# Seven block products in place of eight for one 512x1024x1024 projection, with the weight sums made on GpSimd

## What is computed

```python
a = nsa_attention(...) @ w_branch_attn               # 512 -> 1024
b = pool_mixer(u_pool, ...) @ w_branch_pool          # 512 -> 1024
ga, gb = jnp.split(jax.nn.sigmoid(g_merge), 2, axis=-1)
x = x + (ga * a + gb * b) @ w_out                    # the second output projection, 1024 -> 1024
h = rms_norm_2(x, norm_mlp)
return x + jnp.square(jax.nn.relu(h @ w_ff1)) @ w_ff2
```

## Time and profile before

| | |
|---|---|
| three runs | 1021.49, 1021.76, 1024.25 us |
| profiled execution: its own time | 1022.31 us |
| its span in the trace | 1020.3 us |
| PE busy | 1006.6 us of the span |
| second output projection, first matmul to the first one of the MLP | 637.40 to 683.63 us |
| split tiles of the MLP, to the first whole one | 683.63 to 698.17 us |

### The profile page before, as it was taken

How to read it: one execution, slowest core, us unless ns; L and a number is a source line. 1 busy time by engine, 2 the same in 40 slices (tenths; PEclk the granted TensorE clock), 3 DMA queues, 4 the chain that set the end, 5 groups by cost and what they waited for, 6 DMA issues and landing times.

```text
span 1020.3 us, 14242 instructions
## 1 busy us (share of the span) xinstructions
PE 1006.6 (99%) x5158; PEld 827.6 (81%) x5158; DVE 681.2 (67%) x1201; ACT 555.2 (54%) x1013; POOL 419.1 (41%) x403
## 2 busy tenths in 40 slices
PE   9999999999999999999999999999999999999997
PEld 7788877778778898878887788888888888888886
DVE  5678898888984256733577889344323325999997
ACT  7455444777862456544667874224433446554555
POOL 0023012666720003900354520008779865875563
PEclk9999999999999999999999999999999999999999
DMA  9533321337140384132200443249999941443552
GB/s 338 105 98 93 104 62 42 84 84 197 53 175 1 123 282 131 47 98 63 63 2 1 155 164 96 83 134 311 355 356 340 356 168 62 154 136 143 207 186 83
DMA packets 100165, 146.24 MB, mean 143 GB/s; under 512 B 6480, under 2 KB 60496, under 8 KB 100096
## 3 DMA queue, kind: packets, MB, share of 16 engines
q1 hardware_dynamic: 86800, 130.75, 39.6%
q10 hardware_dynamic: 12768, 12.88, 3.9%
q0 software_dynamic: 528, 1.70, 1.0%
HBM read 123.69 MB, written 21.63 MB: 142 GB/s over the span
## 4 chain that ended last, share of the span: by engine, by line
PE 88%; DVE 6%; ACT 2%; issue 1%; DMA 1%; SPq 1%; POOL 0%; ACTq 0%; DVEq 0%
PE bank L968 59%; PE bank L1483 5%; PE bank L1485 5%; PE bank L1484 5%; PE bank L1363 2%; PE bank L1150 2%; PE bank L1372 2%; PE bank L1121 2%; DVE x L2249 1%; PE bank L1386 1%; PE bank L1134 1%; DMA arena<-in_x 1%; DVE stats L2248 1%; DVE u_lo L2151 1%; PE bank L1273 1%
## 5 line engine op out<-in xcount | busy, mean ns | idle before, releaser
L2666 DVE TENSOR_TENSOR w_lo<-wring,w_hi 128x1024 fp32r<-128x1024 f32 x32 | 51.4, 1607 | 107.5 <-ACT w_hi L2004 107.5
L2151 DVE TENSOR_TENSOR u_lo<-wring,u_hi 128x1024 fp32r<-128x1024 f32 (+2 forms) x69 | 83.3, 1215 | 52.8 <-ACT u_hi L1657 52.3
L968 PE MATMUL bank<-u_hi,h_hi 128*128 128x512 f32 (+1 forms) x288 | 110.9, 385 | 0.0
L968 PE MATMUL bank<-u_hi,h_lo 128*128 128x512 f32 (+1 forms) x288 | 109.2, 379 | 0.0
L968 PE MATMUL bank<-u_lo,h_hi 128*128 128x512 f32 (+1 forms) x288 | 109.0, 378 | 0.0
L1657 ACT ACTIVATE u_hi<-wring 128x1024 fp32r<-128x1024 f32 (+1 forms) x64 | 66.0, 1033 | 70.4 <-PE bank L968 54.5
L968 PE MATMUL bank<-h_hi,w_hi 128*128 128x512 f32 (+2 forms) x272 | 103.2, 379 | 0.0
L968 PE MATMUL bank<-h_hi,w_lo 128*128 128x512 f32 (+2 forms) x272 | 103.1, 379 | 0.0
L968 PE MATMUL bank<-h_lo,w_hi 128*128 128x512 f32 (+2 forms) x272 | 103.1, 379 | 0.0
L968 PE MATMUL bank<-h_hi,u_hi 128*128 128x512 f32 x224 | 93.4, 417 | 0.4 <-ACT arena L1599 0.2
L968 PE MATMUL bank<-h_hi,u_lo 128*128 128x512 f32 x224 | 88.2, 394 | 0.0
(11 more groups left out here) (401 smaller groups left out, 2596.6 us busy)
## 6 DMA issues: line engine op xcount, KB each, us to landing
wring<-in_w_in SPq DMA_DIRECT2D x60, 512.0 KB, 3.9
wring<-in_w_ff ACTq DMA_DIRECT2D x12, 1024.0 KB, 8.5
wring<-sums_kept SPq DMA_DIRECT2D x16, 768.0 KB, 4.2
wring<-in_w_ff SPq DMA_DIRECT2D x22, 512.0 KB, 6.3
wring<-in_w_ff SPq DMA_DIRECT2D x32, 256.0 KB, 3.3
sums_kept<-wring SPq DMA_DIRECT2D x22, 256.0 KB, 5.2
wring<-in_w_out SPq DMA_DIRECT2D x2, 2048.0 KB, 13.0
wring<-in_w_ff SPq DMA_DIRECT2D x4, 1024.0 KB, 6.9
```

Of the source, the lines that this page charges most:

```text
L968: last = mm(b, lhs, rhs, start=(start and n == 0), stop=(stop and n == 2))
L2151: done = v.tensor_tensor(u_lo[raw_place(u)][:, cols], raw_unit(u)[:, cols], u_hi[hi_place(u)][:, cols].bitcast(F32), ALU.subtract)
L2666: v.tensor_tensor(cut(w_lo[ring3(m)]), src, cut(w_hi[ring3(m)]).bitcast(F32), ALU.subtract).then_inc(w_lo_done, 1)
```

## The change

The projection C = A W, with A the mixed activations (two halves of 256 tokens, two halves of 512 inner rows) and W cut into four quarters B11, B12, B21, B22 of 512x512, is made with seven products instead of eight (Winograd's form of Strassen's scheme). With A11, A12 the two inner halves of the first 256 tokens and A21, A22 those of the last: S1 = A21+A22, S2 = S1-A11, S3 = A11-A21, S4 = A12-S2; T1 = B12-B11, T3 = B22-B12, T2 = B22-T1, T4 = B21-T2. The products, in the order in which PE makes them, are B11 with A11, T2 with S2, T1 with S1, B22 with S4, B21 with A12, T3 with S3, T4 with A22. Each has two tiles of tokens (t = 0, 1), four chunks and three matmuls: 24 matmuls of 512 columns, 168 in all.

*Weight sums.* POOL makes T1, T2, T3 and T4 under the first output projection, in eight sets of 512 KB. SP loads a set into one of three places, POOL makes four sums of 128x256, SP stores the set in DRAM (`sets_kept`), waits for the store, and loads the next set into that place. All of this stands in SP's list ahead of the loads of the second layer, and in POOL's list ahead of three memsets for the second layer. The quarters are read back during the branch products.

*Sides.* S1 to S4 are made by DVE (`side_work`, in 256 columns) in the last four rounds of the branch loop, and split by ACT and DVE like the other operands.

*Adds.* A product adds into up to three of the four blocks of x. DVE adds the banks, ACT copies the first product to a running sum, and POOL adds the running sum to x (`add_running`, six adds of 128x512).

*MLP.* The first two tiles are split in 256 and 256 columns, and the transposes of tokens 256 to 511 come inside them.

```diff
@@ SP @@
+            def load_set(s):
+                by_half = lambda a: a.rearrange("p (n c) -> p n c", n=2)[:, :, s % 2 * 2 * P:(s % 2 + 1) * 2 * P]
+                for h in range(2):
+                    row = (4 * h + s // 2) * P
+                    sp.dma_start(set_place[s % SET_PLACES][:, 2 * h:2 * h + 2, :], by_half(w["w_out_2"][row:row + P, :])).then_inc(set_in[s % SET_PLACES], 16)
+            def keep_set(s):
+                sp.wait_ge(set_summed, SET_SUMMED + 4 * (s + 1))
+                sp.dma_start(sets_kept[s].rearrange("p (q c) -> p q c", q=4), set_place[s % SET_PLACES]).then_inc(set_kept[s % SET_PLACES], 16)
...
+                    for s in range(SETS):
+                        keep_set(s)
+                        if s + SET_PLACES < SETS:
+                            sp.wait_ge(set_kept[s % SET_PLACES], SET_KEPT + 16 * (s // SET_PLACES + 1))
+                            load_set(s + SET_PLACES)
...
+                        if e == 3:
+                            sp.wait_ge(last_lo_done, 2)
+                            load_quarter("T1")
+                        elif e == 5:
+                            load_quarter("B21")
+                        elif e == 6:
+                            sp.wait_ge(mix_done, 4)
+                            load_quarter("T2")
+                        elif e == 7:
+                            load_quarter("T3")
+                            load_quarter("T4")
@@ PE @@
+            def out2(name, t):
+                if name in out2_behind:
+                    pe.wait_ge(r_free, out2_behind[name] + t)
+                q = seven.index(name)
+                for j in range(4):
+                    if t == 0 and j % 2 == 0:
+                        pe.wait_ge(w2o_lo_done, low_count(name, j // 2))
+                    if isinstance(out2_sides[name], str):
+                        if t == 0 and j == 0:
+                            pe.wait_ge(side_lows, SIDE_LOWS + ("S2", "S1", "S4").index(out2_sides[name]) + 1)
...
+                        if t == 0 and name in ("B11", "B21"):
+                            pe.wait_ge(m_lo_done, (0 if name == "B11" else 4) + j + 1)
...
+            for name in seven:
+                for t in range(2):
+                    out2(name, t)
+                if name == "T3":
+                    for i in range(2):
+                        h3(i)
...
+            ff_tile(0, 0, 2 * P, range(3))
+            h3(2)
+            ff_tile(0, 0, 2 * P, range(3, KC))
+            h3(3)
...
+            ff_tile(1, 0, 2 * P)
             pe.wait_ge(h_lo_done, halves("h3", NT - 1, 1) + 1)
             for c in range(2):
-                ff_tile(c, 3 * P, S).then_inc(a_full, 1)
+                ff_tile(c, 2 * P, S).then_inc(a_full, 1)
@@ ACT @@
+                quarter_high(*EARLY_HIGHS[e])
+                if e >= 4:
+                    act.wait_ge(mix_done, e + 1)
+                    run(m_hi[e][:, :], gaT[:, e, :], ACT.Copy).then_inc(m_hi_done, 1)
+                    act.wait_ge(side_sums, SIDE_SUMS + 3 * (e - 4) + 2)
+                    run(m_hi[e - 4][:, :], gaT[:, e - 4, :], ACT.Copy).then_inc(m_hi_done, 1)
@@ DVE @@
+            def side_work(j):
+                upper, lower, other = gaT[:, j, 0:2 * P], gaT[:, j, 2 * P:S], gaT[:, j + 4, 2 * P:S]
+                s1, s2 = side_part(side_raw["S1"], j), side_part(side_raw["S2"], j)
+                dve.wait_ge(mix_done, j + 5)
+                v.tensor_tensor(s1, lower, other, ALU.add).then_inc(side_sums, 1)
+                v.tensor_tensor(lower, upper, lower, ALU.subtract).then_inc(side_sums, 1)
+                dve.wait_ge(side_sums, SIDE_SUMS + 3 * j + 1)
+                v.tensor_tensor(s2, s1, upper, ALU.subtract).then_inc(side_sums, 1)
+                mixed2_low(j)
...
+            LOW_AT = {1: (("B11", 0),), 2: (("B11", 1),), 3: (("B22", 0),), 6: (("T2", 0),), 7: (("T2", 1), ("T1", 0))}
...
+                if e >= 4:
+                    side_work(e - 4)
+                for name, h in LOW_AT.get(e, ()):
+                    quarter_low(name, h)
@@ POOL @@
+            for s in range(SETS):
+                pool.wait_ge(set_in[s % SET_PLACES], 32 * (s // SET_PLACES + 1))
...
+                g.tensor_tensor(b11, b12, b11, ALU.subtract).then_inc(set_summed, 1)
...
+            all_kept(pool)
             pool.wait_ge(xn_done, NT)
...
+            def add_running(i, n, t):
+                xs = x[:, i, n * 512:(n + 1) * 512]
+                g.tensor_tensor(xs, xs, running[t], ALU.add).then_inc(running_added, 1)
```

More of the change, by code:

```diff
@@ L134, in weight_groups @@
     groups += [("block2", [])]
-    groups += [(f"w2o{n}", [cols(w["w_out_2"], 512 * n, 512)]) for n in range(2)]
+    groups += [(f"w2o{n}", []) for n in range(2)]
     return groups
@@ new lines, in build @@
+        side_hi = {name: half(f"side_hi{n}", SIDE, ("hT", n * SIDE)) for n, name in enumerate(("S1", "S2", "S4"))}
+        running = [wring[:, 3 * SLOT + S * t:3 * SLOT + S * (t + 1)] for t in range(2)]
+        side_part = lambda a, j: a[:, 2 * P * j:2 * P * (j + 1)]
+        HIGHS = ("B11", "B22", "T1", "T2", "B21", "T3", "T4")
+        high_count = lambda name, h: 2 * HIGHS.index(name) + h + 1
+        LOWS = [("B11", 0), ("B11", 1), ("B22", 0), ("T2", 0), ("T2", 1), ("T1", 0), ("T1", 1), ("B22", 1)]
@@ L506, in build @@
+        LOWS += [(name, h) for name in ("B21", "T3", "T4") for h in range(2)]
+        low_count = lambda name, h: LOWS.index((name, h)) + 1
+        SETS, SET_PLACES = 8, 3
+        set_place = [region(4 * 2 * P, at).rearrange("p (q c) -> p q c", q=4) for at in (strips_at, strips_at + 8 * P, zT_at + 2 * S)]
+        set_slot = {"T1": 0, "T3": 1, "T4": 2, "T2": 3}
         unit_at = [16384, 18560, 18560 + 2 * D]
@@ L957, in t_bank, with three @@
                 return bank[4 + n % 2]
-            def three(b, weights, cols, act, rows, weights_first, start, stop, terms=range(3)):
+            def three(b, weights, cols, act, rows, weights_first, start, stop, terms=range(3), low_at=None):
                 (w_high, w_low), (a_high, a_low) = weights, act
+                low_cols = cols if low_at is None else slice(low_at, low_at + cols.stop - cols.start)
                 for n, (wt, a) in enumerate(((w_high, a_high), (w_high, a_low), (w_low, a_high))):
@@ L964, in three @@
                         continue
[L965 removed]
+                    lhs, rhs = wt[:, low_cols if n == 2 else cols], a[:, rows]
                     if not weights_first:
@@ new lines, in _ @@
+            out2_behind = {"B11": R_OUT2 - 1, "B21": out2_used("T2") - 1, "T3": out2_used("T2") - 1, "T4": out2_used("T3") - 1}
+            def out2(name, t):
[8 more added lines that the diff above has]
+                            pe.wait_ge(side_lows, SIDE_LOWS + ("S2", "S1", "S4").index(out2_sides[name]) + 1)
+                        side = side_hi[out2_sides[name]], side_lo[out2_sides[name]]
+                        rows = slice((2 * j + t) * P, (2 * j + t + 1) * P)
+                    else:
+                        highs, lows, at = out2_sides[name]
+                        if t == 0 and name in ("B11", "B21"):
+                            pe.wait_ge(m_lo_done, (0 if name == "B11" else 4) + j + 1)
+                        side = highs[j], lows[j]
+                        rows = slice(at + t * P, at + (t + 1) * P)
+                    last = three(bank[out2_bank[name] + t][:, :], (w2o_hi[q % 4], w2o_lo[name, j // 2]), slice(512 * j, 512 * (j + 1)), side, rows,
+                                 False, j == 0, j == 3, low_at=j % 2 * 512)
+                last.then_inc(r_full, 1)
@@ L1449, in _, with ff_tile @@
             h3 = lambda i: h_transposes("h3", xn3, 2 * NT, [i])
-            residual(R, ready2, product2, h3)
-            R += 2 * NT
-            def ff_tile(c, first, end):
-                for k in range(KC):
+            def ff_tile(c, first, end, chunks=range(KC)):
+                for k in chunks:
                     last = three(bank[AT[("ff", c)] % 2][:, first:end], (w_hi[ring3(c)], w_lo[ring3(c)]), slice(k * P, (k + 1) * P),
@@ new lines, in out2_add @@
+            def out2_add(name, t):
+                part = bank[out2_bank[name] + t][:, :]
+                dve.wait_ge(r_full, R_OUT2 + 2 * seven.index(name) + t + 1)
+                xs = lambda i, n: x[:, i, n * 512:(n + 1) * 512]
+                if name == "T2":
+                    dve.wait_ge(first_copied, FIRST_COPIED + t + 1)
+                elif name == "T3":
+                    dve.wait_ge(running_added, RUNNING_ADDED + t + 1)
+                elif name == "T1":
+                    v.tensor_tensor(xs(2 + t, 1), xs(2 + t, 1), part, ALU.add)
+                    dve.wait_ge(running_added, RUNNING_ADDED + t + 1)
+                elif name == "B22":
+                    dve.wait_ge(r_free, out2_used("T1") - 1 + t)
+                elif name == "B21":
+                    dve.wait_ge(r_free, out2_used("B11") - 1 + t)
+                elif name == "T4":
```

(3 more changed lines are left out.)

279 lines of the change are left out of this document (211 added, 68 removed).

## The result

Eight runs of the changed kernel have a median of 1023.92 us (1023.12 to 1025.81), eight of the kernel before 1021.62. The ratio is 1.0021, with an interval of 1.0012 to 1.0030. The forecast was 1020.8, that is 1.0 us faster. The time lies in the range, and within 0.3% of before, but on the other side, and the interval leaves out no change.

A forecast was written before the change was run, and what follows sets the result against it. It took PE's own list as the bound. Gross gain 7.7 less entry 2.9, transfers 1.3, T2 1.2 and tail 1.3 left 1.0 us less, forecast as 1020.8 us; range 1017.0 to 1024.4.

The forecast's parts named there:

- The gross gain of 7.7 us: PE's list: 24 fewer matmuls in the second output projection, 5.45 us, and the MLP tiles cut at 256 columns, 2.25.
- the entry wait: Before B11's fourth chunk: PE waits 2.9 us for DVE's low part, behind the last gate, S1 and S3; 1.8 to 3.3.
- the wait at T2: Before product T2: PE waits 1.2 us for S2's low part on DVE, 0.6 to 1.3; sign: ended by L2850.
- the sets and the third `kwvg` unit: Eight weight-sum sets ahead of the second layer's loads: cost nothing, at most 0.6 us; no PE wait for that unit.
- a wait at (4, 1) behind T1's load: Sign in the timeline: a PE wait of 1 to 2 us at branch product (4, 1), ended by its weights' low part.
- The late set loop: Rival: stores landing in 7.5 us, not 4.7, make the third `kwvg` unit 7 us late; 6 slower, 1026.8; chance 0.07.
- the tail, term (4): From T4's end into the MLP: waits before transposes and last low part, 1.3 us; floor 0.5, ceiling 2.5 with GpSimd contention.
- term (2): Transfers: T1's 1 MB ahead of branch piece 4 delays product (4, 1); rows give 1.5 us, 1.3 taken, 0 to 2.6.
- The clock was a rival: Rival: behind the entry wait the clock drops to 1.2 of 2.4 GHz for 24 matmuls; 4.4 slower, 1026.2; chance 0.05.
- a slice below full: Sign that the prediction was wrong: a granted clock below full in any slice of the profile.

The follow-up runs named there:

- experiment 2: Changed kernel with GpSimd's four last adds (running sums into x, tokens 256 to 511) cut from 512 to 8 columns: 1022.48 us, ratio 1.0010.
- experiment 1: Changed kernel with T1's 1 MB load issued behind branch piece 4, not ahead of it: 1022.33 us, ratio 1.0007.
- experiment 7: Changed kernel with the edits of experiment 6 together with T1's load behind branch piece 4: 1022.53 us, ratio 1.0006.
- experiment 5: Changed kernel with 26 more useless 512-column matmuls on PE, set in front of four of its waits: 1023.29 us, ratio 1.0014.
- Experiment 3: Changed kernel with A11's fourth chunk split into high and low parts two rounds earlier, so B11 no longer waits for S3: 1024.18 us, ratio 1.0023.
- experiment 6: Changed kernel with A11's fourth chunk split early and DVE's list behind the last gate set by need, S2 first: 1023.42 us, ratio 1.0019.
- version 12: Experiment 9's kernel with T4's first add before the second h_lo pair, the second MLP tile's weight low part later, two early running adds on DVE: 1018.16 us.
- experiment 10: Experiment 9's kernel with all six running adds on DVE and none on GpSimd: 1020.62 us, ratio 0.9985.
- experiment 9: Experiment 7's kernel with norms and T3's first add ahead of the MLP's weight differences, and one of B22's earlier: 1019.63 us, ratio 0.9977.

## Why the prediction was wrong

*What held.* The gross gain of 7.7 us; the entry wait, 2.73 for 2.9; the wait at T2, 1.13 for 1.2, ended by the low part of S2 (L2856; the L2850 that the prediction names, and that ends DVE's list in the section on the change, is S4 ahead of it); the sets and the third `kwvg` unit, hidden; a wait at (4, 1) behind T1's load. The late set loop did not happen; 6 slower would have been 1027.8 and not 1026.8.

*The step that failed is the tail, term (4).* It was put at 1.3 with a ceiling of 2.5, and it was 3.74. The sum took the add, the norm and the transposes as the tail's chain and found short waits there. The runs show another: DVE's first two differences of h_lo, which the first MLP tile needs, at 1.61 us each beside GpSimd's adds (0.64 alone, experiment 2), a wait of 1.66, and 1.7 us at the lower clock behind it. The row for the contention was at hand, 2.19 for 1.22 in the earlier trace rows, but the 1.3 holds nothing for it: it was given to "two or three DVE steps of the tail" in the ceiling alone, and to none that PE waits for ahead of the first tile.

The Trainium skill, "GPSIMD Engine Reference", section "1. Specifications", names VectorE instructions with two SBUF inputs among those that contend with GpSimd, and experiment 2 agrees on both sides: the differences slow down by 2.5 times, the takes from PSUM not at all.

*The second is the size of term (2).* The rows gave 1.5 us and I took 1.3; the wait was 2.50. Piece 4 came at 614.85, for a forecast of 614.8, but that was luck: this whole execution ran 0.8 us ahead of before's, piece 3's issue (602.57 for 603.40 in the earlier trace rows) as well as PE at product (4, 1) (617.22 less the wait is 614.7, for 615.64 in the earlier trace rows). So T1 cost more than its 3.5 us of transfer. Without it ahead, in experiment 1, piece 4 is there at 610.24, in an execution that ran another 0.25 us earlier: T1 cost 4.4. Of that 1.3 is SP, which issues T1's two halves first and gets to piece 4 that much later (605.50 for 603.91); the sum had nothing for it.

*The clock was a rival and came as a part.* I gave it 0.05 as an alternative, behind the entry. It came behind the wait in the tail, 1.7 us; the prediction's sign for it, a slice below full, could not have shown it, but the finer view does. Of the versions that left PE a wait of 1.6 us or more, all but one (experiment 7) have a fall somewhere in the profiled execution. It belonged into the sum as a cost that one of the waits would bring.

The Trainium skill, "TensorE: Matmul & The Clock Gate", section "Why this matters for your kernels", warns of idle gaps between bursts of matmuls; the falls behind PE's waits, and the full clock of experiment 5, agree with that. Why the fall came behind the wait of 1.66 us and not behind the longer ones, no run here shows.

*What was not looked at.* The waits were priced one by one against PE's list. Experiment 3 shows that the two in front of T2 were one chain through DVE, and experiment 6 that a wait taken away there can come back further on. DVE was busy for 17.73 us before and 38.28 after in the same 40 us, and a sum of the DVE instructions that the change adds there would have shown that it has no time left in which a late step could be made up. That its load as such holds PE up is not shown: version 12 is as full, and PE idles for 0.6 us.

## What to carry to other kernels

When a change takes work from the bounding engine and gives it to another, sum that other engine's work over the stretch, not only the steps that PE meets; near full, its order decides, and single edits (experiments 3 and 6) show little while all together gave 0.6 to 0.7%. An add on GpSimd beside DVE's two-input differences is not free for DVE; beside steps that read PSUM it was (experiment 2), so that would be the place to try. Moving such adds to DVE gave no clear gain (experiments 10 and 12). Count a wait of PE with what the clock may lose behind it.

## What the runs showed of the hardware

The clock's fall was not where I expected it. In the changed kernel it came behind the wait of 1.66 us and not behind those of 2.50 and 2.73; in experiment 1 behind 3.5, in experiment 3 behind 3.7, and there it lasted for more than 6 us, as it did in experiment 10 (two rows of the view by stretch, with the clock behind the busy times):

```profile
648.00:652.00 4.00, 3.37 (x8) 2.75 (x9) 4.00 (x6) 1.56 (x3) 0.00 (x0) 0.50 0.00 0
652.00:655.00 3.00, 3.00 (x9) 2.35 (x9) 1.96 (x3) 2.48 (x3) 0.04 (x1) 0.56 0.00 0
```

With the same wait of 2.0 us before the first MLP tile, experiment 6 had a fall behind it and experiment 7 none. No profiled execution had two falls between 580 and 720 us. What decides at which wait it falls stays open.

One profiled execution can't tell what a version's clock does, as executions of one kernel differ in it. In experiment 7 four executions with a mean granted clock of 0.998 or more took 1021.2 to 1021.9 us, seven with 0.997 took 1022.4 to 1023.2. In experiment 9 those with 0.999 took up to 1019.1, those with 0.997 from 1020.1 up; in experiment 10 five with 0.999 took up to 1020.0, and three with 0.995 took 1022.2 to 1022.6. In experiments 1 and 2 the times don't follow the clock as clearly.
